# Token norms of a fused transformer kernel: squares of the last four tokens tiles one by one, two of eight low parts on VectorE, first output weights of the MLP scaled earlier

## The reference, cut to what matters

```
for l in range(2):
    mod = silu(c) @ w_mod[l] + b_mod[l];  sh1, sc1, gt1, sh2, sc2, gt2 = split(mod, 6)
    h = rms_norm(x, g_norm_mix[l]) * (1 + sc1) + sh1
    ... attention of two kinds on h @ w_in[l] ...
    x = x + gt1 * (concat(o_dil, o_mla) @ w_out[l])
    h = rms_norm(x, g_norm_mlp[l]) * (1 + sc2) + sh2
    x = x + gt2 * (square(relu(h @ w_mlp_in[l])) @ w_mlp_out[l])
```

## Time and profile before

| what | value |
|---|---|
| median of three runs | 4099.81 us (4095.04, 4099.81, 4099.94) |
| the profiled execution | 4095.74 us, span 4093.9 us |
| PE busy | 3830.1 us, 94% of the span |
| DVE, ACT, POOL busy | 51%, 37%, 40% |
| granted TensorE clock, mean | 0.975 of full |

### The profile page before, as it was taken

One profiled execution on the slowest core, in us unless ns is written; L12 is line 12 of the kernel. 1 busy time (PEld: TensorE's weight loads), 2 busy tenths in 40 slices (PEclk: granted clock), 3 DMA queues, 4 the chain that ended last, 5 costly groups with the idle time before them and its releaser, 6 DMA issues.

```text
span 4093.9 us, 52729 instructions
## 1 busy us (share of the span) xinstructions
PE 3830.1 (94%) x19336; PEld 3199.5 (78%) x19336; DVE 2105.4 (51%) x3607; ACT 1532.6 (37%) x2777; POOL 1652.1 (40%) x1426
## 2 busy tenths in 40 slices
PE   6999798889898999998999999897999998999999
PEld 4888677777786888777888888786888787888887
DVE  4453587613665767644444542665767643233233
ACT  3221466622433766622212122433766622222221
POOL 5442146522553620035444444553620035444442
PEclk9999899999999999999999999999999999999999
DMA  5765755331256431122323221256422121111111
GB/s 182 221 185 147 164 141 120 83 128 57 100 133 177 109 74 47 47 87 93 110 87 83 94 81 42 105 133 180 108 70 52 42 95 58 52 41 52 52 42 57
DMA packets 285848, 402.32 MB, mean 98 GB/s; under 512 B 43892, under 2 KB 206836, under 8 KB 285044
## 3 DMA queue, kind: packets, MB, share of 16 engines
q1 hardware_dynamic: 278680, 373.79, 32.1%
q10 hardware_dynamic: 6912, 25.17, 2.2%
HBM read 311.60 MB, written 96.45 MB: 100 GB/s over the span
## 4 chain that ended last, share of the span: by engine, by line
PE 71%; issue 8%; POOL 7%; DVE 6%; POOLq 2%; ACT 2%; DVEq 1%; DMA 1%; SPq 1%; ACTq 0%
PE ps L488 6%; PE ps L490 6%; PE ps L489 6%; PE ps L2400 5%; PE ps L2402 5%; PE ps L2401 5%; PE ps L2418 5%; PE ps L2420 5%; PE ps L2419 5%; PE ps L1882 3%; POOL WL L437 2%; POOL rs L875 2%; PE ps L1526 2%; PE ps L1527 1%; PE ps L1536 1%
## 5 line engine op out<-in xcount | busy, mean ns | idle before, releaser
L437 POOL TENSOR_TENSOR WL<-RAW,WH 128x1024 fp32r<-128x1024 f32 x226 | 556.0, 2474 | 727.0 <-ACT WH L419 716.9
L488 PE MATMUL ps<-WH,XTh 128*128 128x512 f32 (+1 forms) x1536 | 616.7, 402 | 62.0 <-POOL WL L437 40.0
L490 PE MATMUL ps<-WL,XTh 128*128 128x512 f32 (+1 forms) x1536 | 603.2, 393 | 0.0
L489 PE MATMUL ps<-WH,XTl 128*128 128x512 f32 (+1 forms) x1536 | 602.9, 392 | 0.0
L419 ACT ACTIVATE WH<-RAW 128x1024 fp32r<-128x1024 f32 x226 | 234.5, 1061 | 788.2 <-PE ps L2420 361.4
L2440 DVE TENSOR_TENSOR X<-ps,X 128x512 f32<-128x512 f32 x512 | 349.3, 689 | 256.6 <-PE ps L2420 255.6
L2418 PE MATMUL ps<-WH,Hh 128*128 128x512 f32 x1024 | 402.7, 393 | 15.0 <-issue 10.9
L2400 PE MATMUL ps<-XTh,WH 128*128 128x512 f32 x1024 | 401.6, 392 | 14.9 <-issue 11.6
L2431 DVE TENSOR_TENSOR MT<-ps,MT 128x512 f32<-128x512 f32 x128 | 88.5, 692 | 625.7 <-ACT MT L2454 625.7
L2401 PE MATMUL ps<-XTl,WH 128*128 128x512 f32 x1024 | 400.3, 391 | 0.0
L2402 PE MATMUL ps<-XTh,WL 128*128 128x512 f32 x1024 | 400.1, 391 | 0.0
(11 more groups left out here) (257 smaller groups left out, 7806.0 us busy)
## 6 DMA issues: line engine op xcount, KB each, us to landing
RAW<-w_all SPq DMA_DIRECT2D x232, 512.0 KB, 3.5
WM<-w_mod ACTq DMA_DIRECT2D x48, 512.0 KB, 4.2
WM<-w_mod SPq DMA_DIRECT2D x48, 512.0 KB, 3.8
QKd<-KA_d SPq DMA_DIRECT2D x64, 256.0 KB, 5.7
QKm<-QM_d SPq DMA_DIRECT2D x32, 384.0 KB, 4.7
X_d<-X SPq DMA_DIRECT2D x2, 4096.0 KB, 12.0
QKd<-QA_d SPq DMA_DIRECT2D x16, 512.0 KB, 3.5
X<-X_d SPq DMA_DIRECT2D x2, 4096.0 KB, 13.0
```

Source lines behind the costliest of these rows:

```text
L437: e.tensor_tensor(w_low(n), w_raw(n), w_high(n).bitcast(F32), ALU.subtract).then_inc(w_ready, 1)
L488: e.matmul(bank, a, w, start=(kc == 0), stop=False)
L489: e.matmul(bank, b, w, start=False, stop=False)
L490: j = e.matmul(bank, a, l, start=False, stop=(kc == K - 1))
```

## The change

`LOW_SHARE = 6`: of the eight low parts of a half, POOL takes the first six and DVE the last two, behind its `shift` of group 7 (in `out_product` behind the last addition to X). The squares of tiles 4 to 7 are taken one by one between the `high` instructions of the first half, into a tile beside (`GT` or the new `SQJ`, with a drain of ACT between them), in all norms but the first. In the third and fifth norm a second buffer `GTN` gets `gt2` at the start of `out_product`; POOL scales pieces 2 and 3 with it there, splits piece 2 ahead of `roots` of the second half and piece 3 behind them. In step 0 of the MLP, pieces 4 and 5 are split behind k = 1, groups 8 to 15 are transposed together behind k = 1, and k = 2 waits group by group. In pj2 the transposes move one tile ahead. In the last step of the MLP of layer 0 the transposes move from behind second products 13 and 15 to 10 and 12, `scale` from 11 to 9, and `shift` from 14 and the end to 11 and 13.

```diff
+        SQJ = sb("SQJ", [P, D], c=c3)
+        sb("Hh_rest", [P, D], c=c3)
+        GTN = sb("GTN", [P, D], c=c3)
...
+        def first_gate_row(who, L):
+            if who.key == "sp":
+                who.e.dma_start(GTN[:], GT_d[L, 1:2, :].to_broadcast([P, D])).then_inc(gate_loaded, 16)
+            if who.key == "pool":
+                who.e.wait_ge(gate_loaded, 32 * L + 16)
... nt:
                     if who.key == "dve":
                         nm.shift(e, 0, KC)
+                        nm.low(e, LOW_SHARE, KC)
                         prepare_constants(e)
                 if who.key == "act":
-                    nm.squares(e, 1)
                     if led is None:
+                        e.wait_ge(NORM["full"], KC)
+                        nm.squares(e, 4, 8)
                         prepare_functions(e)
                     nm.high(e, KC, n_g)
                 if who.key == "pool":
                     nm.roots(e, 1)
-                    nm.low(e, KC, n_g)
+                    if scaled(first + 3):
+                        w_split_low(e, first + 3)
+                    nm.low(e, KC, KC + LOW_SHARE)
                 if who.key == "dve":
                     nm.scale(e, 1)
                     nm.shift(e, KC, n_g)
+                    nm.low(e, KC + LOW_SHARE, n_g)
... Normed:
+                self.beside = None if L == 0 else GT if L % 2 else SQJ
+            def square(self, e, t):
+                if self.final is not None:
+                    e.wait_ge(*self.final(t))
+                if t > 4 and self.beside is not None:
+                    e.drain()
+                junk = XN[:, t % 4, :] if t < 4 or self.beside is None else self.beside[:]
+                i = e.activation(junk, self.src[:, t, :], ACT.Square, accum_out=ss1[:, t:t + 1])
+                if t % 4 == 3:
+                    i.then_inc(self.s["sq"], 1)
... low:
+                    if kc >= LOW_SHARE:
+                        e.wait_ge(self.s["lo"], self.n0 + n)
... proj_pe:
-                if n in (1, 2):
-                    pj.turned.groups(e, KC + 4 * n - 4, KC + 4 * n)
+                m = n - 1 if pj.mod else n
+                if m in (0, 1):
+                    pj.turned.groups(e, KC + 4 * m, KC + 4 * m + 4)
... out_product, act:
-                    nm.squares(e, 0)
-                    nm.high(e, 0, KC)
+                    nm.squares(e, 0, 4)
+                    for t in range(4, T):
+                        nm.high(e, 2 * t - 8, 2 * t - 6)
+                        if t == T - 1:
+                            w_split_high(e, first + N_OUT + 2)
+                        nm.square(e, t)
+                    w_split_high(e, first + N_OUT + 3)
... out_product, pool:
                     early(who, first + N_OUT, 0, 2)
+                    first_gate_row(who, gated)
+                    for n in (first + N_OUT + 2, first + N_OUT + 3):
+                        w_scale(e, n, GTN)
                     nm.roots(e, 0)
-                    nm.low(e, 0, KC)
+                    nm.low(e, 0, LOW_SHARE)
+                    w_split_low(e, first + N_OUT + 2)
... out_product, dve, at its end:
+                if nm is not None:
+                    nm.low(e, LOW_SHARE, KC)
... gate, act:
                     if n == 15:
+                        nm.squares(e, 4, 6)
                         nm.high(e, 0, 4)
-                nm.high(e, 4, KC)
+                nm.square(e, 6)
+                nm.high(e, 4, LOW_SHARE)
+                nm.square(e, 7)
+                nm.high(e, LOW_SHARE, KC)
... mlp_step, pe:
-                        if step == 0 and k == 2:
-                            turned.ready(e, 1)
                         for kc in range(KC):
+                            if step == 0 and k == 2:
+                                turned.ready_group(e, KC + kc)
-                        if step == 0 and half == 0:
-                            turned.groups(e, KC + 4 * et, KC + 4 * et + 4)
+                        if step == 0 and k == 1:
+                            turned.groups(e, KC, 2 * KC)
-                        if nm is not None and k in (13, 15):
-                            nm.turned.groups(e, 2 * k - 26, 2 * k - 22)
+                        if nm is not None and k in (10, 12):
+                            nm.turned.groups(e, 2 * k - 20, 2 * k - 16)
... mlp_step, dve:
-                    if nm is not None and k == 11:
+                    if nm is not None and k == 9:
                         nm.scale(e, 0)
-                    if nm is not None and k == 14:
-                        nm.shift(e, 0, 4)
+                    if nm is not None and k in (11, 13):
+                        nm.shift(e, 2 * k - 22, 2 * k - 18)
                 if nm is not None:
-                    nm.shift(e, 4, KC)
+                    nm.low(e, LOW_SHARE, KC)
... mlp_step, act and pool, step 0: pieces 4 and 5 behind k == 1 in place of the step's start
... mlp_step, act, last step of layer 0:
-                    nm.squares(e, 0)
-                    nm.high(e, 0, KC)
+                    nm.squares(e, 0, 5)
+                    for t in range(5, T):
+                        nm.high(e, 3 * t - 15, min(3 * t - 12, KC))
+                        nm.square(e, t)
```

More of the change, by code:

```diff
@@ L67 @@
 MOD_LAG = 5
+LOW_SHARE = 6
 PJ_TILES = 2 * 512 + 3 * 512 + 2 * ST_SLOTS * 512
@@ L419, in w_split_high, with w_scale @@
             e.activation(w_high(n), w_raw(n), ACT.Copy).then_inc(w_rounded, 1)
-        def w_scale(e, n):
+        def w_scale(e, n, gate=GT):
             e.wait_ge(w_loaded[n % RAW_SLOTS], 16 * (n // RAW_SLOTS) + 16)
-            e.tensor_tensor(RAW[:, n % RAW_SLOTS, :], RAW[:, n % RAW_SLOTS, :], GT[:], ALU.mult).then_inc(w_scaled, 1)
+            e.tensor_tensor(RAW[:, n % RAW_SLOTS, :], RAW[:, n % RAW_SLOTS, :], gate[:], ALU.mult).then_inc(w_scaled, 1)
         def gate_row(who, L):
@@ L583, in __init__, with squares @@
                 self.turned = Turned(NORM, L, src, True)
[L585 to L592, removed]
+            def square(self, e, t):
[7 more added lines that the diff above has]
+                    i.then_inc(self.s["sq"], 1)
+            def squares(self, e, first, end):
+                for t in range(first, end):
+                    self.square(e, t)
             def roots(self, e, g):
@@ L652, in groups, with ready_group @@
                     i.then_inc(self.s["full"], 1)
+            def ready_group(self, e, n):
+                e.wait_ge(self.s["hi"], self.n0 + n + 1)
+                e.wait_ge(self.s["lo"], self.n0 + n + 1)
             def ready(self, e, g):
@@ L2086, in out_product @@
                     early(who, first + N_OUT, 0, 2)
+                    first_gate_row(who, gated)
+                    for n in (first + N_OUT + 2, first + N_OUT + 3):
+                        w_scale(e, n, GTN)
                     nm.roots(e, 0)
-                    nm.low(e, 0, KC)
+                    nm.low(e, 0, LOW_SHARE)
+                    w_split_low(e, first + N_OUT + 2)
             if key == "sp" and nm is not None:
-                early(who, first + N_OUT, 0, 2)
+                early(who, first + N_OUT)
             if key == "pe":
@@ L2362, in mlp_step, with next_high, next_low @@
             nm = norm_of(3) if last and L == 0 else None
+            def next_high():
+                for n in (n0 + 4, n0 + 5):
+                    w_split_high(e, n, guarded=(step == 0))
+            def next_low():
+                for n in (n0 + 4, n0 + 5):
+                    w_split_low(e, n)
             if key == "sp":
@@ L2377, in mlp_step @@
                     e.wait_ge(s["yfull"], ys)
-                for n in (n0 + 4, n0 + 5):
-                    w_split_high(e, n, guarded=(step == 0))
-            if key == "pool" and more:
-                for n in (n0 + 4, n0 + 5):
-                    w_split_low(e, n)
+                    next_high()
+            if key == "pool" and more and step:
+                next_low()
             if key == "pe":
```

10 lines of the change are left out of this document (5 added, 5 removed).

## The result

The changed kernel takes 4079.08 us (median of 5 runs, 4077.72 to 4080.67), the kernel before 4099.81 in the same session (5 runs, 4095.04 to 4100.83): a ratio of 0.9948 with a 95% interval of 0.9937 to 0.996, faster by about 20.7 us, or half a per cent. The forecast was 4080 in 4067 to 4090. Span of the profiled execution: 4077.3 us, against 4093.9 before.

The account below looks back on a forecast made before the run. PE, busy 94% of the span, was taken as the bound, losing time in stops around the norms, largely through POOL's late queue. Terms +1.1 - 3.0 - 5.7 - 6.5 - 5.7 = -19.8 us gave 4080, range 4067 to 4090.

Parts of the forecast that it names:

- Third and fifth norm: Around the third and fifth norm, to the end of MLP step 0: gain 5.7 us each, bounds 3.5 to 10.
- The stop ahead of k = 0: Third and fifth norm: DVE's low part waits for one whole POOL split, so PE starts 3.5 us later, at 1843.9.
- the 1 us taken for low clock: Step 0 in third and fifth norm, k = 2 and 3: 1 us added for low clock, bounds 0 and 2.5.
- rival (c): Step 0, third and fifth norm: k = 2 waits group by group, clock stays low; 4118 us, chance 0.04.
- Rival (d): The change doesn't do what it says, because POOL is still last; near 4096 us, chance 0.07.
- Rival (a): Third and fifth norm: DVE and POOL miss each other, PE stops only 2.8 us; 4072 us, chance 0.18.
- First norm: First norm: low parts on DVE delay `prepare_constants` and tile 0's heads; loss 1.1 us, bounds 0 and 2.
- Second norm: Second norm and the projection behind it: gain 3.0 us, bounds 0.5 and 4.
- PE's own work then lasts until 1087.2 ... gain 1.0 + 2.0: Second norm's projection: PE's work replaces a stop until 1088.2 and the low clock behind it; gain 3.0 us.
- rival (b): Second and fourth norm's projections: late heads and weights take back 3.5 of 6.5 and all the second's; 4086, chance 0.13.
- Fourth norm: Fourth norm and its projection: the 4.7 us stop and its low clock go; gain 6.5 us, bounds 3 and 8.
- Tile 4 ends at 2622.2 in place of 2628.7: Fourth norm's projection: without the stop ahead of tile 4, that tile ends earlier; gain 6.5 us.

Follow-up runs that it names:

- the second experiment: Changed kernel with pieces 2 and 3 of the MLP's first step scaled and split after the norm again, as before: 4089.95 us.
- The first experiment: Changed kernel with POOL taking all eight low parts, DVE none, in the third and fifth norm's first half: 4068.98 us.
- narrow splits: Changed kernel with POOL's low part cut to 64 of 1024 columns for four projection weight pieces per layer, results left wrong: 4071.24 us.
- the first trace: Unchanged kernel before, the profiled execution the forecast started from: span 4093.9 us.
- the second trace of before: Unchanged kernel before, profiled once more in the last experiment: span 4100.9 us, ratio to itself 1.0002.

## Why the prediction was right, and where it was not

The time was right, and the mechanism of its largest part; two terms were not, and that the sum still came out is in part luck.

**Third and fifth norm: right.** Forecast 5.7 us each, measured 6.05 and 6.15 against the trace that the forecast started from. The stop ahead of k = 0 was to be 5.1 us and was 5.17, by the cause named: the low parts wait for one split. Only the order differs, the split came first by 0.2 us and the roots between them were stretched too. k = 0 and 1 were to take 13.3 us and took 13.67; from there to the second products 20.1 were forecast and 19.1 measured, since the 1 us taken for low clock did not come. The second products were to start at once, and did, with the clock back at 1.00, so rival (c) fell: products 2 and 3 ran at 0.90 through their waits. Rival (d) fell too. Rival (a), a stop of 2.8 us if the two engines did miss each other, was sized right: the second experiment takes the split away and the stop is 3.0. The first experiment goes further, takes VectorE's share away and measures 4068.98.

The Trainium skill, GPSIMD Engine Reference, section Key points, names VectorE instructions with two SBUF inputs among those that collide with GpSimd. The trace agrees: 3.64 us for two low parts beside a split, 1.48 without. The swing of the clock that the Trainium skill tells of in TensorE: Matmul & The Clock Gate, section A second HAM failure mode: psum-queue depth-cycling, for short pauses between groups of matmuls cost little here; the clock read 0.90 in the broken stretch.

**First norm: right as far as it can be told.** Forecast a loss of 1.1 us; the stop ended at 74.60 in place of 74.16, and on average over eight traces with this code 1.05 later. The forecast laid all of it on VectorE's share; without the share 0.4 us of it are left, so that cause is not shown.

**Second norm: wrong in size.** Forecast a gain of 3.0 us, bounds 0.5 to 4; measured 0.6 ahead of the projection and 0.2 in it. The step that failed is "PE's own work then lasts until 1087.2 ... gain 1.0 + 2.0". The stop ahead of tile 4 did go, but PE came to tile 4 only 0.05 us sooner, counted from the norm's start, so the 1.0 was not there; the 2.0 of low clock was, and tile 4 ended 2.0 us sooner. But I let that gain run on to the end of the projection without asking whether the weights follow. They did not: 1.6 of the 2.0 us were gone at the end of tile 8, where PE now waits three times 0.7 us for a split in place of once, and with narrow splits these waits are gone. This is rival (b), at nearly its full price in this norm.

**Fourth norm: wrong twice.** Forecast 6.5 us, 0.9 of it ahead of the projection. There the changed kernel lost 1.3 in its trace (38.17 against 36.85), and up to 2.8 in others: PE's new stop of 2.1 us at product 10 was foreseen, the clock of 0.89 over the broken stretch behind it was not. Counted from the step's first second product, the first `shift` came 1.1 us sooner where 2.9 were forecast, and the last one ended 0.7 us later than before; behind it DVE still had the two evictions and two low parts that the forecast had counted. In the projection the gain was 2.1 us against the first trace and 6.2 against the second. The step "Tile 4 ends at 2622.2 in place of 2628.7" held inside the projection (5.5 us by the end of tile 4, where 5.6 were forecast; 4.2 counted from the norm's start), and then the gain was given back: 1.2 us in tile 8, 2.2 in the stop for rotated heads that the first trace of before did not have. Only because the second trace of before has that stop as well does the average gain come to some 4.2 us. How often the kernel before has that stop, two traces cannot say.

**The sum.** With the mean of the two traces of before (span 4097.4) the changed kernel's 4077.3 is 20.1 us less: 13.1 from the third and fifth norm (12.2 against the first trace alone), about 4.2 from the fourth's projection less 1.3 ahead of it, 0.8 from the second, less 0.4 at the head. That makes 16.3. The rest, some 4 us, lies in stretches without an edit, the first block and layer 0's attention, which differ by 2 to 5 us from trace to trace; the steps of the MLPs between those with a norm agree to 0.1 us. So the forecast's 19.8 came out, but 9.5 us of its terms brought about 3.7, the third and fifth norm brought 1.7 more than forecast, and some 4 us no run ties to the change. To that extent the agreement is luck.

What stays open: why the old order of the last MLP step, shorter by 1.2 us or more in its own stretch, never shows in the time; and how much each of the smaller edits of the third and fifth norm brings.

## What to carry to other kernels

Before a short VectorE instruction with two SBUF inputs is put beside GpSimd work to spare GpSimd, ask what GpSimd does at that moment: here the two low parts together cost one whole weight split and two small rotation instructions one each, and the engine with the longer list would have been done sooner by itself. A gain at one tile is not a gain until the queue that feeds the later tiles has been followed to the end of the stage. And a trace of before is one execution: where the forecast leans on a stop of 2 us, look for the same stop in the same stage of another layer, as the second and fourth norm offered it here.

## What the runs showed of the hardware

- GpSimd and VectorE take turns by whole instructions where VectorE's operands lie in SBUF, and length doesn't matter to the one that waits: a VectorE multiplication of 32 elements per partition took 2.41 us beside weight splits and 0.18 alone. GpSimd waits as well: its root instructions of 4 elements took 0.53 and 1.46 us in place of 0.20 and 1.01, and splits 2.86 in place of 2.36.
- A VectorE instruction that reads one of its operands from PSUM did not wait. Groups of the changed kernel (count, busy us, mean ns): the MLP's addition from PSUM took 0.689 us each in 512 instructions, of which 217 ran almost wholly beside GpSimd work, with the same mean; the addition of `out_product`, both operands in SBUF, took 0.956 on average and 0.69 alone.

```profile
L2493 DVE TENSOR_TENSOR X<-ps,X 128x512 f32<-128x512 f32 x512 | 349.1, 689 | 255.6 <-PE ps L2473 254.4 <-issue 0.2
L2161 DVE TENSOR_TENSOR X<-MT,X 128x512 f32<-128x512 f32 x32 | 30.6, 956 | 3.0
```

- The low clock behind a stop of PE does not go by the stop's length alone. Tile 0 of the fourth norm's projection (24 matmuls, 4.78 us at full clock, 2.4 GHz) took 6.10 us behind a stop of 5.05 us, 7.44 behind 5.27, 6.75 and 7.04 behind two of 5.6, 7.11 behind 6.71, and 6.60 behind 7.26. Behind a stop of some 1.84 us ahead of k = 0 the clock stayed at 1.00 in six cases and read 0.87 over the next 12.8 us in two. What a stop costs in clock is read from several traces, not from one.
